# One level of Strassen's scheme in the key and value projection of a sparse-attention and state-space decoder step

## The reference, cut to what matters

```python
def nsa_project(xn, w_in, pos):
    b, t = xn.shape[0], xn.shape[1]
    proj = jnp.einsum('btd,de->bte', xn, w_in)
    q = proj[..., :Q_W].reshape(b, t, N_HEADS, HEAD_DIM)
    kv = proj[..., Q_W:Q_W + 6 * KV_W].reshape(b, t, 6, N_KV_HEADS, HEAD_DIM)
    gates = jax.nn.sigmoid(proj[..., Q_W + 6 * KV_W:].astype(jnp.float32)).astype(xn.dtype)
    gates = gates.reshape(b, t, N_HEADS, 3)
    return (q, rope(q, pos), gates, kv[:, :, 0], kv[:, :, 1], rope(kv[:, :, 2], pos), kv[:, :, 3],
            rope(kv[:, :, 4], pos), kv[:, :, 5])
```

## Time and profile before

| what | value |
|---|---|
| median of 3 runs | 1558.99 us (1552.8 to 1560.25) |
| the profiled execution's own time | 1560.04 us |
| its span, first to last instruction | 1558.4 us |
| mean granted TensorE clock | 0.982 of full speed |
| TensorE busy | 96% of the span |
| VectorE, ScalarE, GpSimdE busy | 54%, 27%, 23% |
| stage_project, start of the next stage | at 174.72 us |

### The profile page before, as it was taken

How to read it: one execution, slowest core, us unless ns; L and a number is a source line. 1 busy time by engine, 2 the same in 40 slices (tenths; PEclk the granted TensorE clock), 3 DMA queues, 4 the chain that set the end, 5 groups by cost and what they waited for, 6 DMA issues and landing times. The chain is left out here.

```text
span 1558.4 us, 25165 instructions
## 1 busy us (share of the span) xinstructions
PE 1491.9 (96%) x9415; PEld 1199.8 (77%) x9415; DVE 844.3 (54%) x1893; ACT 418.1 (27%) x1061; POOL 359.8 (23%) x488
## 2 busy tenths in 40 slices
PE   8999999788889989999999999899999999999998
PEld 7734799545554878888888888678888888888886
DVE  3332143677634578555567643780385556676513
ACT  3011233677721063333410000333351111000001
POOL 0000300355562218997000008362000000000000
PEclk9999799899998999999999999999999999999999
DMA  6447472210099632644443321523122313322201
GB/s 217 131 134 165 124 211 68 76 34 2 2 294 356 159 124 97 214 158 153 151 135 122 122 82 34 216 110 116 55 67 97 108 54 109 108 82 81 82 27 55
DMA packets 141515, 184.31 MB, mean 118 GB/s; under 512 B 31322, under 2 KB 99618, under 8 KB 140370
## 3 DMA queue, kind: packets, MB, share of 16 engines
q1 hardware_dynamic: 137586, 172.21, 33.8%
q0 software_dynamic: 3808, 10.49, 2.0%
HBM read 163.42 MB, written 29.69 MB: 124 GB/s over the span
## 5 line engine op out<-in xcount | busy, mean ns | idle before, releaser
L2399 POOL TENSOR_SCALAR att_p<-att_p,att_tot,gates 128x512 f32<-128x512 f32 (+3 forms) x128 | 79.7, 635 | 67.1 <-DVE att_tot L2321 67.1
L294 PE MATMUL psum<-xT,l_w 128*128 128x260 f32 x384 | 85.6, 383 | 6.1 <-ACT nsa_y L493 2.9
L1646 PE MATMUL psum<-proj_w,xT 128*128 128x512 f32 x192 | 90.7, 606 | 0.0
L948 PE MATMUL psum<-xT,l_w 128*128 128x260 f32 x384 | 85.2, 383 | 1.6 <-PEq L113 1.6
L294 PEld LDWEIGHTS psum<-xT,l_w 128*128 128x128 f32 x384 | 72.7, 190 | 17.9 <-issue 3.5
L948 PEld LDWEIGHTS psum<-xT,l_w 128*128 128x128 f32 x384 | 72.8, 190 | 12.9 <-issue 1.8
L1972 PE MATMUL psum<-cmp_xt,cmp_w 64*128 64x256 f32 (+2 forms) x640 | 79.8, 394 | 0.4 <-DVE cmp_xt L1896 0.4
L964 PE MATMUL psum<-l_up_t,l_w_sums 128*128 128x260 f32 x336 | 78.2, 382 | 0.0
L2314 DVE CUSTOM_DVE_ANT_0 att_p<-psum,causal 128x512 f32<-128x512 f32 (+3 forms) x128 | 57.4, 486 | 35.5 <-PE psum L2160 35.0
L2369 ACT ACTIVATE att_p<-att_p,att_low 128x512 f32<-128x512 f32 (+3 forms) x128 | 70.8, 556 | 4.6 <-DVE att_low L2314 4.1
L964 PEld LDWEIGHTS psum<-l_up_t,l_w_sums 128*128 128x128 f32 x336 | 63.8, 190 | 9.8
(11 more groups left out here) (551 smaller groups left out, 3126.1 us busy)
## 6 DMA issues: line engine op xcount, KB each, us to landing
l_w<-in_mlp_w SPq DMA_DIRECT2D x16, 2048.0 KB, 8.1
l_w<-in_mlp_w SPq DMA_DIRECT2D x32, 1024.0 KB, 4.8
proj_w<-in_nsa_w_in SPq DMA_DIRECT2D x4, 2048.0 KB, 9.1
sa_more<-in_cache_kv_sel POOLq DMA_DIRECT2D x52, 128.0 KB, 7.9
cmp_raw<-in_cache_kv_cmp SPq DMA_DIRECT2D x24, 256.0 KB, 3.0
xT<-in_cache_kv_cmp SPq DMA_DIRECT2D x24, 256.0 KB, 3.1
sa_more<-in_cache_kv_sel SPq DMA_DIRECT2D x44, 128.0 KB, 10.3
hT<-in_cache_kv_cmp SPq DMA_DIRECT2D x16, 256.0 KB, 2.9
```

The lines of the kernel that those rows point to most:

```text
L294: mm = nc.tensor.matmul(ps[:, n % 8, 0:HALF], w[s][:, k, m * P:(m + 1) * P], src[:, kk, cols(h)], start=(kk == 0), stop=(kk == last))
L948: mm = nc.tensor.matmul(ps[:, n % 8, 0:HALF], w[s][:, k, m * P:(m + 1) * P], src[:, kk, cols(h)], start=(kk == 0), stop=(kk == last))
L1646: mm = nc.tensor.matmul(ps[:, bank_of(step), :], c.xT[:, k, t * P:(t + 1) * P], w[:, i % 2, k, :], start=(k == 0), stop=(k == KD - 1))
L2399: ve.tensor_scalar(pr[:, n % PR, par, 0:w], pr[:, n % PR, par, 0:w], tot[:, n % PR, par:par + 1], c.gates[:, i, gate:gate + 1], ALU.mult, ...
```

## The change

Per key and value block the 512 x 1024 by 1024 x 512 product (tokens, features, columns) is cut into halves in all three dimensions and made by seven half products in place of eight, in Winograd's form. Each half product is two token tiles by four feature tiles, 8 products of 256 columns. The four sums of input halves are made once, by VectorE, between query steps, over the parked `hT`; the four sums of weight halves are made per block, the first block's behind head pair 6. VectorE joins the products into `c.kv` by seven operations per block, and ScalarE scales the joined tiles in place. All gates stand in bank 6, and are evicted together at the end. The store of `hT` moves ahead of the swaps, and VectorE waits for it ahead of the first eviction. TensorE waits for `s5_kept` and for all query evictions ahead of the first half product. The diff, cut:

```diff
@@ sync @@
                 sp.dma_start(wg[:], w_in[:, :, nblk * NG:]).then_inc(gate_landed, 16)
+                sp.wait_ge(h_kept, 2 * (QT + 1))
+                sp.dma_start(c.scratch_h, c.hT[:].rearrange("p k t -> p (k t)")).then_inc(c.h_stored, 16)
+
                 def swap_q(m):
...
-                sp.wait_ge(h_kept, 2 * (QT + 1))
-                sp.dma_start(c.scratch_h, c.hT[:].rearrange("p k t -> p (k t)")).then_inc(c.h_stored, 16)
@@ tensor @@
+                    mm = nc.tensor.matmul(ps[0:n, 6, t * 3 * NH:(t + 1) * 3 * NH], c.xT[:, k, t * P:t * P + n], wg[:, k, :],
                                           start=(k == 0), stop=(k == KD - 1))
...
+                def kv_product(bank, left, right, gates):
+
+                    for t in range(2):
+                        for k in range(KH):
+                            mm = nc.tensor.matmul(ps[:, bank, t * KVW:(t + 1) * KVW], left[:, k, t * P:(t + 1) * P], right[:, k, :],
+                                                  start=(k == 0), stop=(k == KH - 1))
+                            if gates:
+                                gate_product()
+                    mm.then_inc(kv_filled, 1)
...
                 pe.wait_ge(gate_landed, 16)
+                pe.wait_ge(s5_kept, 2)
                 for i in range(3):
+                    gates = i == 2
                     pe.wait_ge(landed[i % 2], 16 * (i // 2 + 2))
+                    if i == 0:
+                        pe.wait_ge(q_kept, nq)
+                    else:
+                        pe.wait_ge(row_kept, i)
+                    kv_product(0, x_part(0, 0), w_part(i, 0, 0), False)
+                    row_parts(i)
+                    if i >= 1:
+                        pe.wait_ge(kv_joined, 7 * i)
+                    kv_product(5, x_part(0, 1), w_part(i, 1, 0), gates)
+                    pe.wait_ge(x_summed, 4)
+                    pe.wait_ge(w_summed, 4 * i + 2)
+                    kv_product(1, x_s[:, 1], w_s3[:, 1], gates)
...
+                    nc.tensor.matmul(ps[0:NB, 0, :], sel[:], parts, start=True, stop=True).then_inc(row_filled, 1)
+                    pe.wait_ge(w_summed, 4 * i + 3)
+                    kv_product(2, x_s[:, 2], w_s3[:, 2], gates)
+                    kv_product(3, x_s[:, 0], w_s3[:, 0], gates)
+                    pe.wait_ge(w_summed, 4 * i + 4)
+                    kv_product(4, x_part(1, 1), w_s4, False)
+                    pe.wait_ge(kv_joined, 7 * i + 1)
+                    kv_product(5, x_s[:, 3], w_part(i, 1, 1), False)
@@ scalar @@
+                    for at, t in enumerate((2, 3, 0, 1)):
+                        act.wait_ge(kv_joined, 7 * i + 6 + at // 2)
+                        nc.scalar.mul(c.kv[:, t, b, :], c.kv[:, t, b, :], rs_tok[:, 0, t:t + 1]).then_inc(kv_scaled, 1)
+                act.wait_ge(gates_filled, 1)
+                for t in range(QT + 1):
...
+                    nc.scalar.activation(c.gates[0:n, t, :], ps[0:n, 6, t * 3 * NH:(t + 1) * 3 * NH], ACT.Exp, scale=rs_tok[0:n, 1, t:t + 1])\
+                        .then_inc(gates_kept, 1)
@@ vector @@
+                def sum_w(i):
+
+                    dve.wait_ge(landed[i % 2], 16 * (i // 2 + 2))
+                    if i >= 1:
+                        dve.wait_ge(kv_filled, 7 * i - 1)
+                    nc.vector.tensor_sub(w_s3[:, 0], w_part(i, 0, 1), w_part(i, 0, 0)).then_inc(w_summed, 1)
...
+                    for n, (out, old, product, bank) in enumerate(JOINS):
+                        if n == 6 and i < 2:
+                            sum_w(i + 1)
+                        dve.wait_ge(kv_filled, 7 * i + product)
...
+                        nc.vector.tensor_tensor(corners[out], corners[old], kv_bank(bank), ALU.subtract if product == 6 else ALU.add).then_inc(kv_joined, 1)
...
                 dve.wait_ge(table_landed, 32)
+                dve.wait_ge(c.h_stored, 16)
                 for m in range(KD):
...
+                    if 2 <= m < 6:
+                        sum_x(m - 2)
+                    if m == 6:
+                        sum_w(0)
...
                 for i, b in enumerate(ORDER_KV):
-                    for t in range(QT + 1):
+                    join_kv(i, b)
+                    for at, t in enumerate(TILES_KV):
```

More of the change, by code:

```diff
@@ L1463, in stage_project @@
     gate_landed, table_landed = c.sem("proj_gate_w_landed"), c.sem("proj_table_landed")
-    block_read, filled, freed = c.sem("proj_block_read"), c.sem("proj_bank_filled"), c.sem("proj_bank_freed")
+    block_read, filled = c.sem("proj_block_read"), c.sem("proj_bank_filled")
+    x_summed, w_summed = c.sem("proj_x_summed"), c.sem("proj_w_summed")
+    kv_filled, kv_joined, kv_scaled = c.sem("proj_kv_filled"), c.sem("proj_kv_joined"), c.sem("proj_kv_scaled")
+    first_copied, row_filled, row_kept = c.sem("proj_first_copied"), c.sem("proj_row_filled"), c.sem("proj_row_kept")
+    gates_filled, gates_kept = c.sem("proj_gates_filled"), c.sem("proj_gates_kept")
     q_kept, roped = (c.sem(f"proj_{x}") for x in ("q_kept", "q_roped"))
@@ L1499, in bank_of, with x_part, w_part, kv_part @@
             return (n + 4) % 6
[L1501 to L1507, removed]
+        KH, TH = KD // 2, SEQ // 2
+        TILES_KV = (2, 3, 4, 0, 1)
+        JOINS = ((0, 1, 2, 5), (1, 1, 3, 1), (2, 1, 4, 2), (3, 2, 5, 3), (1, 1, 5, 3), (2, 2, 6, 4), (1, 1, 7, 5))
+        x_s = c.hT[:].rearrange("p k t -> p (k t)")[:, 0:4 * KH * TH].rearrange("p (s k t) -> p s k t", s=4, k=KH)
+        w_s3 = c.place("proj_w_sums", [P, 3, KH, HN], 0)
+        w_s4 = c.qz[:, 1, 0].rearrange("p b x -> p (b x)").rearrange("p (k n) -> p k n", k=KH)
+        def x_part(a, b):
+            return c.xT[:, b * KH:(b + 1) * KH, a * TH:(a + 1) * TH]
+        def w_part(i, a, b):
+            return w[:, i % 2, a * KH:(a + 1) * KH, b * HN:(b + 1) * HN]
+        def kv_part(b, a, n):
+            return c.kv[:, 2 * a:2 * a + 2, b, n * KVW:(n + 1) * KVW]
+        def kv_bank(n):
+            return ps[:, n, :].rearrange("p (t x) -> p t x", t=2)
         with nc.Block() as block:
@@ L1554, in _ @@
                 for i, b in enumerate(ORDER_KV):
-                    for t in range(QT + 1):
-                        sp.wait_ge(roped, 8 + i * (QT + 1) + t + 1)
+                    for n, t in enumerate(TILES_KV):
+                        sp.wait_ge(roped, 8 + i * (QT + 1) + n + 1)
                         if t < QT:
@@ L1568, in _, with start_bank @@
                 step = 0
[L1570 to L1577, removed]
+                def start_bank(k):
+                    if k == 0 and step >= 6:
+                        pe.wait_ge(q_kept, step - 5)
                 def spread_rs():
@@ L1631, in _, with gate_product @@
                 pe.wait_ge(sel_made, 1)
-                def gate_product(t, n, k, ahead):
-                    start_bank(k, ahead)
-                    mm = nc.tensor.matmul(ps[0:n, bank_of(step + ahead), 0:3 * NH], c.xT[:, k, t * P:t * P + n], wg[:, k, :],
-                                          start=(k == 0), stop=(k == KD - 1))
-                    if k == KD - 1:
-                        mm.then_inc(filled, 1)
+                gates_made = 0
+                def gate_product():
+                    nonlocal gates_made
+                    t, k = divmod(gates_made, KD)
+                    n = rows_of(t)
+                    mm = nc.tensor.matmul(ps[0:n, 6, t * 3 * NH:(t + 1) * 3 * NH], c.xT[:, k, t * P:t * P + n], wg[:, k, :],
+                                          start=(k == 0), stop=(k == KD - 1))
+                    gates_made += 1
+                    if gates_made == KD * (QT + 1):
+                        mm.then_inc(gates_filled, 1)
@@ new lines, in kv_product, with row_parts @@
+                def kv_product(bank, left, right, gates):
[6 more added lines that the diff above has]
+                    mm.then_inc(kv_filled, 1)
+                def row_parts(i):
+                    if i >= 1:
+                        pe.wait_ge(parts_kept, i)
+                    for k in range(KD):
+                        q = k % 4
+                        mm = nc.tensor.matmul(ps[32 * q:32 * q + 32, 7, :], c.xT[:, k, T - 32:T], w[:, i % 2, k, :],
+                                              start=(k < 4), stop=(k >= 4), tile_position=(0, 32 * q))
+                    mm.then_inc(parts_summed, 1)
@@ new lines, in _ @@
+                    kv_product(1, x_s[:, 1], w_s3[:, 1], gates)
+                    pe.wait_ge(parts_kept, i + 1)
+                    pe.wait_ge(first_copied, i + 1)
+                    nc.tensor.matmul(ps[0:NB, 0, :], sel[:], parts, start=True, stop=True).then_inc(row_filled, 1)
[3 more added lines that the diff above has]
+                    pe.wait_ge(w_summed, 4 * i + 4)
@@ L1668, in _ @@
                 for k in range(KD):
-                    gate_product(QT, NB, k, 0)
+                    gate_product()
             @block.scalar
@@ L1691, in _ @@
```

(26 more changed lines are left out.)

19 lines of the change are left out of this document (added).

## The result

The changed kernel takes 1570.36 us (median of 7 runs, 1568.45 to 1573.38) against 1555.44 us for the kernel before (7 runs, 1551.17 to 1560.25). The ratio is **1.008, 95% interval 1.006 to 1.0101** (the quotient of the two medians is 1.0096). 1569.7 us was forecast, counted from the median of the kernel before in its first three runs, 1558.99 us. The profiled execution took 1571.78 us with a span of 1570.1 us, 11.7 us more than before, where the sum had 10.7.

A forecast was written before the change was run, and what follows sets the result against it. TensorE, busy in 96% of the span, was taken as the bound. -9.9 + 11.1 + 5.8 + 2.7 + 1.0 = +10.7 us on the profiled 1560.04 gave 1570.7, less 1.05 for the runs' median: 1569.7 us, range 1562 to 1577.

The forecast's parts named there:

- half products: Key and value blocks on TensorE: seven half products for eight, 3.3 us less per block, -9.9 us in three blocks.
- wait at the start: Ahead of half product 1, TensorE waits for VectorE's copies behind rotation 7 and swap 7: +11.1 us.
- clock behind it: After the idle start, TensorE's first work runs at half clock, priced from an earlier 4.88 us stall: +2.7 us.
- stage's end: Behind the last gate product: join, scaling, table load, exponentials, five pairs of 0.65 us and barrier; +5.8 us.
- next stage and rest: Behind the projection: clock already fallen, so the next stage's first 1.9 us run at half speed; +1.0 us (0 to 2).
- the rival of more stalls: Each of 21 half products starts behind a semaphore or another bank, 0.3 us each: +6.3 us, 1576.0 us; chance 0.12.
- One sign: At the start, TensorE's idle time from 72.7 to about 83.8 us would be put down to VectorE's copy of `cols`.
- VectorE's and the store's part: VectorE's added sums and joins cost 0; the moved store, expected near 33 us, costs 0, at most 0.7 us.
- the cheap end: Clock loss after the start's idle time, low estimate: 2.1 us of work at half clock, 1.1 us lost.
- the swap did not overtake the load: Rival at the start: swap 7 lands at 77.4 us ahead of the load, +7.3 for +11.1, 1565.9 us; chance 0.06.
- the clock turned slightly against the change: Rival in the next stage: full clock granted earlier, over 5 us return, all of it 9.9: 1559.8 us; chance 0.07.
- The takeover by the transfer-bound stage: Rival at 460 us: TensorE's later wait for transfers takes up to 4.9 of the 10.7 us, 1564.8 us; chance 0.07.

The follow-up runs named there:

- run 5: Changed kernel with 88 transposes of the identity filling the 11 us that TensorE waits at the start; ratio 1.0067 to the kernel before.
- (1): Changed kernel with the wait for the second s5_kept moved from ahead of the first half product to ahead of the last block's first gate product; ratio 0.9989.
- (4): Kernel before with one wait added, for the second s5_kept ahead of the first key and value product; ratio 1.0086.
- (6): Changed kernel with swap 7 issued ahead of the load of key and value block 1 instead of behind it; ratio 1.0033.
- run 2: Changed kernel with gate products behind half product 5 of the last block, gates evicted and inverted beside half products 6 and 7; ratio 1.0055, 1568.93 us.
- (9): Kernel before, changed kernel, and changed kernel with moved wait and early gates, each profiled again unchanged; half-clock stretches 23.9, 27.3 and 20.5 us.
- both repairs: Changed kernel with the s5_kept wait moved to the last block's first gate product and gates finished beside half products 6 and 7; ratio 0.9961, 1552.94 us.

## Why the prediction was right

The mechanism came as forecast, term by term. That the time itself, 1569.7 against 1570.36 us, agrees to 0.7 us is in part luck. The forecast added 10.7 us to a median of 1558.99, and the kernel before then had 1555.44 over seven runs, so that the two medians are 14.9 us apart. The profiled spans are 11.7 us apart, and those of the second profiles (1568.8 and 1560.2) 8.6.

Against the profiled execution of before, the projection's steps read (forecast, then measured):

| step | forecast us | measured us | from |
|---|---|---|---|
| half products | -9.9 | -9.1 | part of 100.41 us (72.75 to 173.16) against 93.72 (83.58 to 177.30), less 2.4 of clock |
| wait at the start | +11.1 | +10.8 | 83.58 against 72.75 |
| clock behind it | +2.7 | +2.4 | 6.15 us against 3.72, run 5 |
| stage's end | +5.8 | +6.4 | 7.95 us against 1.55 |
| next stage and rest | +1.0 | +1.2 | 11.7 of span less 10.5 |

*Half products.* The slope of 0.83 ns per column held. 0.8 us of the saving went, mostly at the starts of the half products, which I had priced at 0 in the sum and at 6.3 us in the rival of more stalls.
*The wait.* Shown from three sides: taken away (1), put alone into the old kernel (4), shortened through the swap (6). The kernel's other work needed none of it. One sign was wrong: the profile put the wait down to "issue", and to VectorE's `cols` only in run 5.
*VectorE's and the store's part.* Query evictions, sums and joins held nobody (1), and VectorE began at 32.58 us, 0.4 us from the 33 I had named.
*The clock.* Run 5 measured 2.4 us, nearer to the stall row I took than to the cheap end.
*The end.* The mis-sized term: I took pairs of gate operations 0.65 us apart, and with two waits and a semaphore step ahead of each pair they are 0.85 apart (0.71 in run 2, where one wait is left). Run 2 got 5.0 of the 6.4 back.

The rivals: the swap did not overtake the load, in the changed kernel or in runs 4 and 5. In the next stage the clock turned slightly against the change rather than for it. The half-clock stretch is 27.3 us for 20.5, but 4.5 us of it (180.74 to 185.25) lie in idle time; inside the stage it is 22.8 us (to 208.04), 2.3 more than before, and costs some 1.1 us. That meets the +1.0 of the sum, though the stretch is no constant (9), and the table's last row holds more than the clock: the changed kernel is 11.0 us behind at the first scores (293.6 against 282.6), 10.3 at the sample attention's last product (515.1 against 504.8), and 11.7 at the end. That this row came out at 1.2 is luck. The takeover by the transfer-bound stage, to which I gave 0.07, took up no more than those 0.7 us.

The scheme itself is sound: 9 us per execution are saved on TensorE. It was tied to two places where another engine's lag, harmless before, was put on TensorE's path.

## What to carry to other kernels

Where a change reuses a buffer, look up on the old timeline when its last reader ends, not only who it is: here bank 6 was free 11 us late, and the first gate product wants it only at 147.84 us, 64 us after that. Work that is gathered "at the end" (evictions, a table load, short dependent pairs) loses the cover it had; do it as soon as its data are there, beside the last products. And put the wait in front of the first use, not in front of the loop.

## What the runs showed that I had not expected

How the clock fares in the next stage goes with what TensorE does in the gap ahead of it. In all twelve profiles with the gap unfilled (1.55, 2.95 or 7.95 us of idle time) the clock fell within 3 us of the next stage's start, or ahead of it, and the half-clock stretches were 13.7 to 30.7 us. In the two with the gap filled by throwaway transposes it held for 11.3 and 12.7 us, in two kernels, and the stretch was 6.8 us both times. One profile of each filled kernel, and their timed runs, carry this.

In the kernel before this alone is worth 0.4% in timed runs, as much as both repairs of the change. With both repairs and the filler the ratio is 0.9937; its interval and that of the filler alone (0.9948 to 0.9976) overlap, so how much of the 9 us of saved products reaches the end beside it isn't settled.
